# One inference step on one core: the second group's window keys turned by TensorE instead of by the key stream

## The reference

```python
z = h @ p["w_in"]                       # 1056 tokens x 1024 -> 2560 columns: q | k | v | value | gate
# prompt: causal attention, 8 heads of 64, three dilated windows of 128 keys each, combined
# sample: the same windows over cached keys and values, and the new rows
kc = jnp.concatenate([win_k, k], axis=1)   # win_k: 8 x 2048 x 8 x 64
vc = jnp.concatenate([win_v, v], axis=1)
for _, dil in DIL_CONFIGS:              # (128,1), (512,4), (2048,16)
    o_i, l_i = dilated_branch_sample(q, kc, vc, dil)
attn = combine_branches(outs, lses)
...                                     # conv module, output projection, cross-attention, gated ConvFFN
```

## Time and profile before

| | us |
|---|---|
| median of 3 runs | 1795.18 |
| lowest, highest | 1794.22, 1795.99 |
| the profiled execution | 1793.9 |
| its span | 1792.1 |
| TensorE busy in the span | 1690.5 (94%) |
| VectorE, ScalarE busy | 1111.8 (62%), 910.1 (51%) |
| GpSimd busy | 20.8 (1%) |
| mean granted TensorE clock | 0.978 |

### The profile page before, as it was taken

One profiled execution on the slowest core, in us unless ns is written; L12 is line 12 of the kernel. 1 busy time (PEld: TensorE's weight loads), 2 busy tenths in 40 slices (PEclk: granted clock), 3 DMA queues, 4 the chain that ended last, 5 costly groups with the idle time before them and its releaser, 6 DMA issues.

```text
span 1792.1 us, 29564 instructions
## 1 busy us (share of the span) xinstructions
PE 1690.5 (94%) x11614; PEld 1575.9 (88%) x11614; DVE 1111.8 (62%) x2050; ACT 910.1 (51%) x1664; POOL 20.8 (1%) x28
## 2 busy tenths in 40 slices
PE   7999999953999999999999889999999999999998
PEld 7999999732567999988878889999999999999998
DVE  5499997750775587534556667654576543676533
ACT  7444444730566676555456555444545533545533
POOL 0000000012000000000000000000000000000000
PEclk9999999985999999999999999999999999999999
DMA  9999975598631655544443334444444544444443
GB/s 320 225 238 218 214 199 117 195 248 224 243 125 63 182 152 161 164 120 141 123 148 107 105 106 142 135 136 136 136 141 147 151 131 144 130 141 145 145 136 104
DMA packets 417825, 284.02 MB, mean 158 GB/s; under 512 B 69676, under 2 KB 392354, under 8 KB 415888
## 3 DMA queue, kind: packets, MB, share of 16 engines
q1 hardware_dynamic: 412840, 273.31, 53.8%
q10 hardware_dynamic: 4847, 8.83, 1.5%
HBM read 226.97 MB, written 32.48 MB: 145 GB/s over the span
## 4 chain that ended last, share of the span: by engine, by line
PE 74%; DVE 6%; SPq 6%; ACT 5%; DMA 5%; issue 4%; ACTq 0%; POOL 0%; POOLq 0%; DVEq 0%
PE bank L1353 70%; PE bank L1350 4%; DMA raw<-in_w_in_dram 2%; SPq L477 1%; ACT whi L717 1%; SPq L522 1%; SPq L532 1%; SPq L523 1%; ACT WORDS L838 1%; DMA PLANES<-HALVES 1%; DMA raw<-in_w_mv_dram 1%; DVE C L1943 1%; DVE wlo L1956 1%; DMA cached_t<-keys_turned 1%; DVE cv L1943 1%
## 5 line engine op out<-in xcount | busy, mean ns | idle before, releaser
L1353 PE MATMUL bank<-op_hi,whi 128*128 128x352 f32 x1632 | 538.9, 330 | 4.9 <-DVE wlo L1956 2.7
L1956 DVE TENSOR_TENSOR wlo<-raw,whi 128x1024 fp32r<-128x1024 f32 (+1 forms) x312 | 374.1, 1201 | 253.7 <-ACT whi L717 253.2
L1353 PE MATMUL bank<-op_hi,wlo 128*128 128x352 f32 x1632 | 525.3, 322 | 0.0
L1353 PE MATMUL bank<-op_lo,whi 128*128 128x352 f32 x1632 | 524.4, 321 | 0.0
L717 ACT ACTIVATE whi<-raw 128x1024 fp32r<-128x1024 f32 (+1 forms) x312 | 325.1, 1043 | 311.1 <-DMA raw<-in_w_down_dram 82.9
L1353 PEld LDWEIGHTS bank<-op_hi,whi 128*128 128x128 f32 x1632 | 307.2, 188 | 14.5 <-issue 10.1
L1353 PEld LDWEIGHTS bank<-op_lo,whi 128*128 128x128 f32 x1632 | 308.0, 189 | 0.6
L1353 PEld LDWEIGHTS bank<-op_hi,wlo 128*128 128x128 f32 x1632 | 307.2, 188 | 0.0
L1353 PE MATMUL bank<-fhi,whi 128*128 128x352 f32 x528 | 171.1, 324 | 0.0
L1353 PE MATMUL bank<-fhi,wlo 128*128 128x352 f32 x528 | 170.7, 323 | 0.0
L1353 PE MATMUL bank<-h1hi,whi 128*128 128x352 f32 x480 | 159.3, 332 | 0.7 <-DVE wlo L1956 0.7
(11 more groups left out here) (285 smaller groups left out, 2319.2 us busy)
## 6 DMA issues: line engine op xcount, KB each, us to landing
raw<-in_w_up_dram SPq DMA_DIRECT2D x132, 512.0 KB, 3.8
raw<-in_w_down_dram SPq DMA_DIRECT2D x48, 512.0 KB, 4.0
PLANES<-HALVES SPq DMA_DIRECT2D x128, 112.0 KB, 3.6
keys_turned<-WORDS SPq DMA_DIRECT2D x32, 448.0 KB, 3.2
cached_t<-keys_turned SPq DMA_DIRECT2D x8, 1792.0 KB, 9.6
raw<-in_w_out_dram SPq DMA_DIRECT2D x24, 512.0 KB, 4.1
raw<-in_w_xq_dram SPq DMA_DIRECT2D x24, 512.0 KB, 4.1
raw<-in_w_xo_dram SPq DMA_DIRECT2D x24, 512.0 KB, 4.1
```

Source lines behind the costliest of these rows:

```text
L1353: return pe.matmul(out, lhsT, rhs, start=first, stop=last, skip_group_check=shared)
L1956: dve.tensor_tensor(wlo[v % SLOTS][:, 0:nk, :], raw[v % SLOTS][:, 0:nk, :], whi[v % SLOTS][:, 0:nk, :].bitcast(F32), ALU.subtract).then_in ...
```

## The change

The key stream now has 16 pieces (sequences 0 to 3), all of them beside the projections; the old rows of sequences 0 to 2 are gathered by one transfer and those of sequence 3 by another. GpSimd joins nothing. Windows k4 to k7 are loaded raw, as the values are, and in group 1 each slot 0 to 27 turns one tile of 128 keys: TensorE turns it in four blocks into bank 4 or 5 (`key_turn`), ScalarE copies two tiles of three to SBUF and VectorE the third (`KTS`), and a slot later TensorE multiplies it (`key_scores(n)`, 4 matmuls of 128 columns by 32 rows). The scores of sequences 0 to 3 stay as they were (`batch_scores`). While tiles are turned, `product` writes bank 3, one of the two banks of `turn_p`, instead of bank 4. The first three weights of the output projection are issued before the attention, in front of the loads of the bias tables.

```diff
-    PIECES = AT * BD
-    LATE = PIECES - 8
-    PIECES_AT = {u: 1 for u in (*range(NT, 3 * NT, 2), 11, 15, 19, 23, *range(3 * NT, XFIRST), XFIRST)}
+    AHEAD = 4
+    FIRST_TURNED = AHEAD * KTILES
+    PIECES = AT * AHEAD
+    def on_scalar(n):
+        return n % 3 != 0
+    def key_tile(g, r):
+        return g * GROUP + r if 0 <= r < GROUP and (g * GROUP + r) // KTILES >= AHEAD else -1
+    def product_bank(s):
+        return 3 if any(key_tile(*sample_slot(s + 3, pos)) >= 0 for pos in range(3)) else 4
+    PIECES_AT = {u: 1 for u in (*range(NT, 3 * NT, 2), *range(3 * NT, XFIRST - 2))}
...
-            if kind == "k":
+            if kind == "k" and b < AHEAD:
...
-            rows = A["cache_win_v"][0, b].rearrange("s h d -> s (h d)")
+            rows = A["cache_win_v" if kind == "v" else "cache_win_k"][0, b].rearrange("s h d -> s (h d)")
...
-        for u in range(SLOTS, XFIRST):
+        for u in range(SLOTS, XFIRST + SLOTS - 1):
             weight(u)
-            if SLOTS <= u < SLOTS + BD:
-                gather_old(u - SLOTS)
+            if u == SLOTS:
+                gather_old(0, 3)
+            if u == NT + 4:
+                gather_old(3, 4)
...
             if kind == "k":
-                sp.wait_ge(*at("ssc", b))
+                sp.wait_ge(*(at("ssc", b) if b < AHEAD else at("ktr", b * KTILES + KTILES - 1)))
             else:
                 sp.wait_ge(*at("spv", b))
             window(n)
-            if n < 8:
-                for p in range(LATE + 2 * (n - 3), LATE + 2 * (n - 2)):
-                    key_stream(p, LATE, PIECES)
-            if n == 7:
-                for u in range(XFIRST, XFIRST + SLOTS - 1):
...
-                    weight(u)
...
         def sample(g, r):          # ScalarE; VectorE has the same for the other tiles
+            n = key_tile(g, r)
+            if n >= 0 and on_scalar(n):
+                act.wait_ge(*at("ktr", n))
+                if n >= FIRST_TURNED + 2:
+                    act.wait_ge(*at("ssc", ("tile", n - 2)))
+                act.activation(KTS[n % 2][:, :, :], bank[4 + n % 2][:, :].rearrange("p (k n) -> p k n", k=AT), ACT.Copy).then_inc(*mark("ktsa", n))
...
         def product(s):            # TensorE
-            take(4, "att", s)
+            take(product_bank(s), "att", s)
...
+        def key_turn(n):
+            b, a = divmod(n, KTILES)
+            w, c = window_of("k", b)
+            take(4 + n % 2, "ktsa" if on_scalar(n) else "ktsd", n)
+            pe.wait_ge(*at(f"cached{c}", (w, OLD // P - 1)))
+            for k in range(AT):
+                ins = turn(bank[4 + n % 2][:, k * P:(k + 1) * P], cached[c][:, a, k * P:(k + 1) * P])
+            ins.then_inc(*mark("ktr", n))
+        def key_scores(n):
+            b, a = divmod(n, KTILES)
+            g, b = divmod(b, 4)
+            pe.wait_ge(*at("ktsa" if on_scalar(n) else "ktsd", n))
+            for k in range(AT):
+                col = P * (a % 4)
+                ins = mm(bank[6 + a // 4][32 * k:32 * k + 32, col:col + P], QW[:, g, P * b + 32 * k:P * b + 32 * k + 32], KTS[n % 2][:, k, :],
+                         a == 0 and b == 0, b == 3, True)
...
         def sample(g, r):          # TensorE
+            if key_tile(g, r) >= 0:
+                key_turn(key_tile(g, r))
             if r == 1:
                 group_scores(g)
-            if batch_slot(r) >= 0:
-                key_scores(4 * g + batch_slot(r))
+            if key_tile(g, r - 1) >= 0:
+                key_scores(key_tile(g, r - 1))
+            elif batch_slot(r) >= 0:
+                batch_scores(4 * g + batch_slot(r))
```

More of the change, by code:

```diff
@@ L223, in layout @@
     PT = mn("PT", 38912, [P, 2, SEQ])
+    KTS = [mn(f"KTS{i}", 16384 + 2048 * i, [P, AT, P]) for i in range(2)]
     QW = mn("QW", 61440, [P, 2, 544])
@@ L244, in layout @@
     Yb = [mn(f"Y{i}", o, [P, NT, CW]) for i, o in enumerate((50176, 129024, 140288))]
-    STD = [place("STD0", RING + 21504, [P, CW]), place("STD1", RING + 22912, [P, CW]), mn("STD2", 37376, [P, CW])]
+    STD = [place(f"STD{i}", RING + 8192 * i + 4096, [P, CW]) for i in range(CH)]
     SQ = [mn(f"SQ{i}", 129024 + 1408 * i, [P, CW]) for i in range(4)]
@@ L503, in window, with gather_old @@
                 load(dst[:, a, :], rows.rearrange("(g r) n -> g r n", r=16)[a * 32:(a + 1) * 32, 0:4, :], name, (n, a))
[L505 to L510, removed]
+        def gather_old(b0, b1):
+            rows = A["cache_win_k"][0, b0:b1].rearrange("b (g r) h d -> b g r (h d)", r=16)
+            load(A["keys_old"][b0:b1].rearrange("b (g r) n -> b g r n", r=4), rows[:, 0:OLD // 4, 0:4, :], "gathered", b0)
         def turn_keys(p):
@@ L516, in turn_keys @@
                 sp.wait_ge(*at(f"planes{p % 2}", (p - 2, 1, 1)))
-            if k == 0:
-                sp.wait_ge(*at(f"gathered{b % 2}", b))
-            t, name = HALVES[place_of(p)], f"turned{p % 2}"
+            if k == 0 and b % 3 == 0:
+                sp.wait_ge(*at("gathered", b))
+            t, name = HALVES[p % 2], f"turned{p % 2}"
             cols = slice(2 * P * k, 2 * P * (k + 1))
@@ L573, in _ @@
                     load(stage_u[:, i, :], A["state_conv"].rearrange("a b t c -> (a b t) c")[i * 120:(i + 1) * 120, :], "states", ("u", i))
-        for p in range(p, LATE + 2):
-            key_stream(p, 0, LATE)
+        for p in range(p, PIECES + 2):
+            key_stream(p)
         for i in range(2):
-            sp.wait_ge(*at(f"kept{i}", LATE - 2 + i))
+            sp.wait_ge(*at(f"kept{i}", PIECES - 2 + i))
         load(wt[:, :], A["prompt_bias"], "tables", "p")
@@ L692, in _ @@
         pool.memset(QO[:, :, :, :], 0.0).then_inc(*mark("qzw0", 1))
[L694 to L704, removed]
     @block.scalar
@@ L1536, in product, with batch_scores @@
                     h = 2 * hp + e
-                    ins = mm(bank[4][64 * e:64 * e + 64, 0:P], V[:, blk, h * DH:(h + 1) * DH], PT[:, e, blk * P:(blk + 1) * P], blk == 0, blk == i)
+                    ins = mm(bank[product_bank(s)][64 * e:64 * e + 64, 0:P], V[:, blk, h * DH:(h + 1) * DH], PT[:, e, blk * P:(blk + 1) * P], blk == 0, blk == i)
             ins.then_inc(*mark("pv", s))
-        def key_scores(b):
+        def key_turn(n):
[14 more added lines that the diff above has]
+                         a == 0 and b == 0, b == 3, True)
+            ins.then_inc(*mark("ssc", ("tile", n)))
+        def batch_scores(b):
             g, i = divmod(b, 4)
-            n = ORDER_W.index(("k", b))
-            c = n % len(cached)
+            n, c = window_of("k", b)
             pe.wait_ge(*at(f"cached{c}", (n, OLD // P - 1)))
@@ L2166, in sample @@
         def sample(g, r):
+            n = key_tile(g, r)
+            if n >= 0 and not on_scalar(n):
+                dve.wait_ge(*at("ktr", n))
+                if n >= FIRST_TURNED + 2:
+                    dve.wait_ge(*at("ssc", ("tile", n - 2)))
+                dve.tensor_copy(KTS[n % 2][:, :, :], bank[4 + n % 2][:, :].rearrange("p (k n) -> p k n", k=AT)).then_inc(*mark("ktsd", n))
             if r == GROUP + 1:
-                dve.wait_ge(*at("ssc", 4 * g + 3))
+                dve.wait_ge(*at("ssc", 3 if g == 0 else ("tile", 2 * GROUP - 1)))
                 if g:
@@ L2230, in attended @@
             dve.wait_ge(*at("pv", s))
-            dve.tensor_copy(ATT[:, hp, i * P:(i + 1) * P], bank[4][:, 0:P]).then_inc(*mark("att", s))
+            dve.tensor_copy(ATT[:, hp, i * P:(i + 1) * P], bank[product_bank(s)][:, 0:P]).then_inc(*mark("att", s))
         def mix_low(c, m):
```

41 lines of the change are left out of this document (16 added, 25 removed).

## The result

| kernel | median, us | runs, us | span of the profiled execution |
|---|---|---|---|
| before | 1795.31 | 1794.22 to 1795.99 (4) | 1792.1 |
| changed | 1768.75 | 1766.76 to 1769.75 (4) | 1766.0 |

The ratio is 0.9848, with a 95% interval of 0.9836 to 0.9861. That is 27 us faster, where 39 were forecast: inside the range for all outcomes (1746 to 1775), outside the forecast's own range (1748 to 1766), and 12.8 us over the forecast value. The trace says where those 13 us are. I cut each execution into three stretches: up to the first scores of the attention (the first `KT,QT` row of 64x128), the attention, and from the first `op_hi,whi` row on.

The account below looks back on a forecast made before the run. TensorE bounds nearly everywhere, except where late key-stream pieces delay attention windows. -46.9 - 10 + 17.2 + 1.5 + 2 - 1 - 2 = -39.2 from 1793.9 gives 1754.7, median 1756; own range 1748 to 1766 (chance 0.64), all outcomes 1746 to 1775.

Parts of the forecast that it names:

- (a): Attention: TensorE's waits for raw value windows and k4 go once late key-stream pieces leave SP's queue, 46.9 us together.
- (a'): Attention: new waiting for windows v3 and k4, which arrive just in time; +1.5 us, between 0 and 10.
- (b): Attention: TensorE's low clock goes with the waits; 10 us saved, between 8 and 11.
- (c): Group 1: 28 tiles' turns and bursts add 23.8 us, four wide bursts go (6.6); net +17.2, between 13.8 and 23.6.
- (d): Group 1: tile copies mostly covered by TensorE's step; +2 us for late copies and bank 3, between 0 and 28.
- the -1: Attention: TensorE's short waits for VectorE's maxima at a step's start disappear under the tiles; -1 us, between -2 and 0.
- (e): Projections: 8 of 24 pieces and 16 ScalarE joins go; -2 us, between -4 and +3, the plus for the merged gather.
- A: Tiles cost more than their bursts through late copies and the shared bank; +14 to +28, 1770 to 1784 us; chance 0.17.
- B: Attention windows stay late, 3 to 5 us each for four; +12 to +20, 1768 to 1776 us; chance 0.10.
- C: Slower than before: tile copies become a chain behind two exponentials, 59 us exposed, 1815 us; chance 0.05.
- D: Each change between whole-block and quarter-column bursts costs TensorE 0.42 us; 23.5 us, 1780 us; chance 0.04.

Follow-up runs that it names:

- e4: Kernel before without its 8 late key-stream pieces and without tiles; windows k6 and k7 read turned keys of sequences 2 and 3 (wrong keys): 1736.1 us, ratio 0.9676.
- e1: Changed kernel with the old rows of sequences 0 to 2 gathered by three single transfers at the same place instead of one: 1751.63 us, ratio 0.975.
- e11: Changed kernel, still one gather of three sequences, but its loops turned round: 96 groups outermost, sequences inside: 1747.28 us, ratio 0.9727.
- e6: Changed kernel with one gather for each sequence, spread out behind the weights of units 4, 6, 8 and 10: 1748.85 us, ratio 0.9734.
- e8: e6 with the four transposes of every tile in group 1 made twice into the same bank: 1759.3 us, ratio 0.9798.

## Why the prediction was right, and where it failed

**(a), (a'), (b): right.** Waits of 46.9 us were to go and 1.5 to come. The rows have 45.8 + 2.75 before and 2.4 + 1.5 after; the 2.4 is for k3, the window that the forecast named beside v3 and k4, and these two are in time. With the clock the part was put at -55.4, and the kernel with just this edit measures -56.2: 47.5 of idle time, where 45.4 were forecast, and 8.7 of slower work, where 10 were.

**(c), (d): right, a little too dear.** +18.2 forecast, +15.2 measured. TensorE's steps for a tile are 0.04 to 0.1 us longer than assumed, which alone would make 28 x 0.92 - 6.6 = 19.2. Four less than that are paid. The listed waits don't hold them: TensorE waits 3.3 us for VectorE's maxima in e4 and 2.2 in e1, the -1 of the forecast, but 1.0 us for copies comes in. The prompt's own bursts do. Several of its scores take longer in e4 than in e1, here the ones nearest to 426 us, e4 first:

```profile
426.16 1.53 PE L1348 MATMUL bank<-KT,QT 64*128 64x512 f32 x4
```

```profile
426.34 1.13 PE L1342 MATMUL bank<-KT,QT 64*128 64x512 f32 x4
```

Added up from the starts, the scores of 64x512 are 2.5 us shorter in e1 and the turns of `Pp` 1.1. With tiles between them these bursts run without the short stops that they have in e4; what they stop for is not named by the profile. It looks like what the -1 was for, which was then put too small.

**(e): wrong.** The step that failed is "-2, between -4 and +3; the plus is the one gather of 2.3 MB that now stands before early weight loads". Measured is +13.1, made of two parts, and it is the second that was far larger than assumed. Without the merged gather the attention starts 5.6 us earlier than before (e1; 4.2 in e11). The wait of the earlier trace rows shrinks from 3.4 us to 1.5 (2.3 in e11), and the low clock behind it, which the -2 left out, goes. The window from 180 to 240 us of before and of e1 (the clock is the last number but two):

```profile
180.00:240.00 60.00, 56.08 (x340) 55.29 (x339) 58.79 (x48) 27.21 (x42) 0.00 (x0) 0.94 0.88 202
```

```profile
180.00:240.00 60.00, 57.95 (x368) 57.16 (x367) 58.83 (x49) 29.00 (x44) 0.00 (x0) 1.00 0.91 205
```

TensorE is busy 1.9 us longer there, and at full clock. Not all of this is the pieces' doing: e4, which keeps the 24 pieces and the wait of 3.4, has a clock of 1.00 there too and starts at 339.92. Against e4 the fewer pieces are worth 3.8 and 2.4, not far from the -2 and hardly more than the 2.7 between e6 and e8. The merged gather takes +18.7 back. I had priced it by its bytes, as if it ran on all the engines; it ran on three, for some 30 us, and the weight behind it in the queue landed 34.4 us after its issue. The forecast's own test was that stages outside the attention move by no more than 4 us, and it is this that failed.

The Trainium skill (DMA: Bandwidth & Descriptors, section Why a DMA increments its semaphore by 16 and not by 1) states the rule: a transfer gets the largest number of engines up to 16 that divides its slowest dimension on both sides. The trace agrees four times, with shares of 0.13, 0.19 and 0.26 for 2, 3 and 4 sequences outermost, and 1.08, the weights' share included, for 96 groups. The diff showed the outermost loop of three, so that the gather would be slow could have been foreseen. How slow, only these runs show: 2.3 MB at three times 27 GB/s is 29 us.

**The rivals.** A (late copies): TensorE waits 1.0 us in all for a tile's copy by VectorE, and no wait for one by ScalarE is in the list. The time lands near A's 1770, but for another reason; without e1 and e4 one could have taken it for A's proof. B (windows stay late): the time lies inside B's 1768 to 1776 too, but there is one wait of 2.4 us, not four of 3 to 5. C: did not happen. D (a price for each change of shape): the burst behind a turn advances TensorE by 0.36, as a lone burst did before, and 28 tiles cost 15.2 net where D needed over 40. That changing the tiling mode drains TensorE (the Trainium skill, TensorEngine Tiling, section Key Properties) may be so, but no run here shows a drain by itself. What a lone burst costs over its instructions is 0.12 us for four matmuls (0.36 against 0.24 in a long row) and 0.15 for a turn (0.59 against 0.44 for four blocks more in e8), and D needed 0.42 for each.

**What would show it.** Slices 9 and 10 closed (to 8 and 9), the 112 turns and 28 bursts at about the forecast steps, no low clock in group 1: as forecast. The attention was to end near 530; it ended at 540.79, and at 521.81 once the gather was right.

## What to carry to other kernels

Look at the outermost dimension of every transfer that a change adds or merges, before its bytes: two, three or four there cost some 30 us of a nearly empty DMA system here, and putting the long dimension outside took it all back. Price a change of a DMA queue by what is issued behind it: nobody waited for the gather itself at that time, but TensorE waited for the weight behind it. And split the result by stages before explaining a total; the 27 us here are a gain of 41 and a loss of 13, and neither is seen in the sum.

## What the runs showed of the hardware that was not expected

- A DRAM to DRAM copy with 2, 3 or 4 sequences outermost moved 54, 80 and 110 GB/s at a share of 0.13, 0.19 and 0.26, some 27 GB/s for an engine.
- While it ran, the same queue's next two loads took 8.75 and 19.98 us to be issued (0.57 and 0.53 before; 0.37 and 2.99 in e11), and the first of them, a weight of 0.5 MB, landed 34.4 us after its issue began (8.4 before, 13.1 in e11; 33.8 and 34.9 with four and two sequences). What SP and the weight wait for is not shown by the trace.
- A burst of eight turned blocks advances TensorE by 1.03 us (e8), a lone one of four by 0.53 to 0.59: four blocks more are about 0.44, and some 0.1 to 0.15 belongs to the burst, not to its blocks.
